# Expert outputs in a mixture-of-experts kernel: stored to rows of their own and fetched back, in place of adding in memory

## What is computed

```python
def moe_swiglu(h, w_router, w1, w3, w2):
    logits = (h @ w_router).astype(jnp.float32)
    top_val, top_idx = lax.top_k(logits, TOP_K)              # TOP_K = 2 of N_EXPERTS = 8
    top_w = jax.nn.softmax(top_val, axis=-1)
    combine = jnp.sum(jax.nn.one_hot(top_idx, N_EXPERTS) * top_w[..., None], axis=-2)
    out = jnp.zeros_like(h)
    for e in range(N_EXPERTS):
        out = out + combine[..., e:e + 1] * swiglu(h, w1[e], w3[e], w2[e])   # 1024 -> 3584 -> 1024
    return out
...
    x = x + moe_swiglu(h, moe_router[i], moe_w1[i], moe_w3[i], moe_w2[i])
return rms_norm(x, final_g)
```

## Time and profile before

| | |
|---|---|
| median of three runs | 1801.39 us (1799.99 to 1801.99) |
| the profiled execution | 1801.36 us, of which the span 1799.5 us |
| busy in the span | PE 1773.1 us (99%), DVE 1520.6 us (85%), ACT 1222.8 us (68%), POOL 82.7 us (5%) |
| moved | 519.87 MB, mean 289 GB/s |

### The profile page before, as it was taken

How to read it: one execution, slowest core, us unless ns; L and a number is a source line. 1 busy time by engine, 2 the same in 40 slices (tenths; PEclk the granted TensorE clock), 3 DMA queues, 4 the chain that set the end, 5 groups by cost and what they waited for, 6 DMA issues and landing times.

```text
span 1799.5 us, 24857 instructions
## 1 busy us (share of the span) xinstructions
PE 1773.1 (99%) x10081; PEld 1528.1 (85%) x10082; DVE 1520.6 (85%) x1408; ACT 1222.8 (68%) x1138; POOL 82.7 (5%) x97
## 2 busy tenths in 40 slices
PE   9999999999999999999999999999999999999997
PEld 9989898899999989898888877887878877787775
DVE  7999866566557999876579889999999999999996
ACT  5657754454445557754577688888788888888886
POOL 1000000100001000000100010001010010000000
PEclk9999999999999999999999999999999999999998
DMA  8543555345554554454379999999999999999995
GB/s 343 180 173 142 186 188 187 118 164 211 186 182 157 194 178 141 169 223 170 111 284 370 356 414 414 428 426 420 426 404 428 425 422 415 416 427 427 421 414 217
DMA packets 55826, 519.87 MB, mean 289 GB/s; under 512 B 7136, under 2 KB 7392, under 8 KB 12320
## 3 DMA queue, kind: packets, MB, share of 16 engines
q1 hardware_dynamic: 52448, 507.83, 71.1%
q0 software_dynamic: 2544, 9.18, 1.7%
q10 hardware_dynamic: 720, 1.31, 0.2%
HBM read 511.74 MB, written 6.55 MB: 288 GB/s over the span
## 4 chain that ended last, share of the span: by engine, by line
PE 79%; DVE 12%; ACT 4%; DMA 3%; issue 2%; SPq 0%; ACTq 0%; DVEq 0%
PE psum L2119 15%; PE psum L2105 13%; PE psum L2106 12%; PE psum L2107 12%; PE psum L2120 8%; PE psum L2607 6%; PE psum L2608 6%; DVE raw_alias L1355 4%; DVE U_alias L1355 2%; DMA raw<-in_stream 2%; ACT whi L816 2%; DVE wlo L1355 2%; DMA U<-in_stream 1%; PE psum L2620 1%; PE psum L2626 1%
## 5 line engine op out<-in xcount | busy, mean ns | idle before, releaser
L816 ACT ACTIVATE whi<-raw 128x2048 fp32r<-128x2048 f32 (+1 forms) x231 | 436.4, 1897 | 93.1 <-PE psum L2120 50.0
L1355 DVE TENSOR_TENSOR wlo<-raw,whi 128x2048 fp32r<-128x2048 f32 (+1 forms) x144 | 326.2, 2266 | 131.5 <-ACT whi L816 131.2
L2119 PE MATMUL psum<-h_hl,whi 128*128 128x512 f32 x1216 | 429.9, 398 | 0.3 <-DVE U L1713 0.2
L2120 PE MATMUL psum<-h_hl,wlo 128*128 128x256 f32 x1216 | 340.0, 280 | 0.0
L2119 PEld LDWEIGHTS psum<-h_hl,whi 128*128 128x128 f32 x1216 | 228.2, 188 | 55.0 <-issue 1.2
L2120 PEld LDWEIGHTS psum<-h_hl,wlo 128*128 128x128 f32 x1216 | 229.4, 189 | 0.1
L1355 DVE TENSOR_TENSOR raw_alias<-raw,wlo 128x2048 fp32r<-128x2048 f32 x87 | 196.6, 2284 | 18.6 <-ACT wlo L816 18.4
L2105 PE MATMUL psum<-act_hl,whi 128*128 128x256 f32 x720 | 206.2, 286 | 1.1 <-DVE wlo L1355 0.5
L1355 DVE TENSOR_TENSOR raw_alias<-raw,whi 128x2048 fp32r<-128x2048 f32 x87 | 196.6, 2285 | 10.1 <-ACT whi L816 9.7
L2106 PE MATMUL psum<-act_hl,whi 128*128 128x256 f32 x720 | 203.7, 283 | 0.0
L2107 PE MATMUL psum<-act_hl,wlo 128*128 128x256 f32 x720 | 203.6, 283 | 0.0
(11 more groups left out here) (326 smaller groups left out, 3365.4 us busy)
## 6 DMA issues: line engine op xcount, KB each, us to landing
raw<-in_stream SPq DMA_DIRECT2D x87, 2048.0 KB, 18.7
raw<-in_stream SPq DMA_DIRECT2D x141, 1024.0 KB, 4.9
U<-in_stream SPq DMA_DIRECT2D x52, 2048.0 KB, 17.6
memhat<-in_stream SPq DMA_DIRECT2D x29, 1024.0 KB, 14.5
h_hl_alias<-in_stream SPq DMA_DIRECT2D x29, 1024.0 KB, 16.4
raw<-in_stream SPq DMA_DIRECT2D x6, 512.0 KB, 3.5
xacc<-U POOLq DMA_DIRECT2D x3, 512.0 KB, 9.8
xT<-in_x_cols ACTq DMA_DIRECT2D x4, 256.0 KB, 6.5
```

What stands on the lines that cost most here:

```text
L816: act.activation(hi_home(n)[:, 0:words], src[:, 0:words], ACT.Copy).then_inc(hi_ready, 1)
L1355: dve.tensor_tensor(lo_home(n)[:, 0:words], src[:, 0:words], hi_home(n)[:, 0:words].bitcast(F32), ALU.subtract).then_inc(lo_ready, 1)
L2119: pe.matmul(o[:].rearrange("p (a b) -> p a b", a=2), st[0], mv, start=start, stop=False)
L2120: return pe.matmul(o[:, 0:256], st[1], mv[:, 0, :], start=False, stop=stop)
```

## The change

- **Stores.** An expert's rows go plainly to rows of its own in a new array `ys` (1 + 7 x 128 rows). Indices past the end mark empty slots, which `bounds_check` leaves out, in the gathers too. Row 0 is zero. `ys` is cleared by seven transfers of 512 KB that ACT issues at chunks 30 to 36 of layer 1, and one of 4 KB at row 0. The three sends of x to `xacc`, `x_rows` and the first calls of `xrows` are gone.
- **Sums.** `rows_listed` (DVE, n = 16) makes a list `yidx` of four columns: for both blocks of 128 tokens the row of a token's later and earlier expert among p = 0 to 6 (or row 0). `sums_in` gathers two times 128 rows by it, once into `xa` when p = 5 has been sent and once into `xsum` after the store of p = 6 has been issued and has landed. PE turns x of tokens 0 to 127 to rows after step 53, and DVE adds them to `xa` (`kept_added`, n = 323 and 324); x of tokens 128 to 255 is added by PE in `final_rows`, in eight more transposes. DVE adds `xsum` to `xa` in four pieces at n = 325 to 328 (`halves_added`), the first of which waits for the second fetch. `final_rows` and ACT wait for these.
- **Order.** `ALONE` = 5: five big steps, then small and big by turns, then five small. From step 10 on the order is as before.
- **Splits.** Six chunks (`UNDIVIDED`: the first gate chunk of p = 2, 4 and 6 at f = 1 and 4) aren't split: PE takes them as they come in four plain 32-bit matmuls by an unsplit copy of the tokens, `he_full`, and ACT and DVE skip them. So half of the last chunk (`down_last`).
- **Places.** The routing steps move to n = 5, 6, 7, 8, 13, 14, 16 and 21, the slot matrices to 9 to 12, `indices` to step 3. `htok` and `sel` move to the start of `U`, and the two areas of `U` swap roles, so that pair 4 is fetched as soon as the cross attention's scores are done. DVE waits for all of `htok` (`ht_done`) ahead of its first slot matrix.

```diff
-AHEAD = 3
+ALONE = 5
...
-    order, big, small = big[:FSTEPS] + small[:AHEAD], big[FSTEPS:], small[AHEAD:]
-    for pair in zip(big, small):
+    order, big = big[:ALONE], big[ALONE:]
+    for pair in zip(small, big):
         order += pair
...
-    return 4 if s >= FSTEPS else 5
+    return 4 if s >= ALONE else 5
...
+UNDIVIDED = [MOE + gate_end(s) - 1 for s in range(STEPS) if ORDER[s][0] and not few_step(s) and ORDER[s][1] % 3 == 1]
...
+def divided(n):
+
+    return n + 1 - sum(i < n for i in UNDIVIDED)
...
-        htok = u(4096, TB, D)
-        sel = u(6144, TB, NE, SLOTS)
+        htok = u(0, TB, D)
+        sel = u(2048, TB, NE, SLOTS)
...
-        PAIRED = {4: 0, JOINING: 2 * CW}
+        PAIRED = {4: 2 * CW, JOINING: 0}
...
+            sp.wait_ge(xs_done, XH * LAYERS)
+            fetch(4, 0)
...
                 elif q == LOOSE:
+                    sp.wait_ge(w_used, MOE)
+                    fetch_loose(q, 1, 0)
...
-                    sp.wait_ge(ss_done, 6)
-                    sp.wait_ge(ht_done, 4)
+                    continue
...
-                if q == 4:
-                    sp.wait_ge(w_used, MOE)
-                    fetch_loose(LOOSE, 1, 0)
...
-            for t in range(TB):
-                gp.wait_ge(xt_ready, 2 * t + 2)
-                gp.dma_start(xacc[P * t:P * t + P, :], xtok).then_inc(scr_in, 16)
-            gp.dma_start(xacc[S:S + SLOTS, :], xtok).then_inc(scr_in, 16)
...
-                  .then_inc(hg_in, 16)
+                                      in_offset=bass.IndirectOffsetOnAxis(ap=gidx[0:there, p:p + 1], axis=0),
+                                      bounds_check=S - 1, oob_is_err=False).then_inc(hg_in, 16)
+
+            def sums_in(to, first):
+
+                for b in range(TB):
+                    at = first + b
+                    gp.indirect_dma_start(out=to[:, b, :], out_offset=None, in_=ys,
+                                          in_offset=bass.IndirectOffsetOnAxis(ap=yidx[:, at:at + 1], axis=0)).then_inc(xa_in, 16)
...
-                    gp.wait_ge(scr_in, 48)
+                    gp.wait_ge(scr_in, 16 * NE)
+                if e == NE - 2:
+                    gp.wait_ge(ga_done, NE)
+                    sums_in(xa, TB)
                 if e < NE - 1:
                     here = HALF if few(e) else SLOTS
                     gp.wait_ge(y_ev, e + 2)
-                    gp.indirect_dma_start(out=xacc, out_offset=bass.IndirectOffsetOnAxis(ap=sidx[0:here, e:e + 1], axis=0),
-                                          in_=y[0:here, :], in_offset=None, compute_op=ALU.add).then_inc(y_sent, 16)
+                    gp.indirect_dma_start(out=ys, out_offset=bass.IndirectOffsetOnAxis(ap=sidx[0:here, e:e + 1], axis=0),
+                                          in_=y[0:here, :], in_offset=None,
+                                          bounds_check=(NE - 1) * SLOTS, oob_is_err=False).then_inc(y_sent, 16)
                     if e + 3 < NE:
                         rows_in(e + 3)
-            gp.wait_ge(ga_done, NE)
-            gp.dma_start(xa, xacc[0:S, :].rearrange("(b p) d -> p b d", p=P)).then_inc(xa_in, 16)
+            sums_in(xsum, 0)
...
+                    p = n - BASE[1] - CLEARED
+                    if 0 <= p < NE - 1:
+                        act.dma_start(ys[1 + SLOTS * p:1 + SLOTS * p + SLOTS, :].rearrange("p (a b) -> p a b", a=DB),
+                                      ones[:].unsqueeze(1).to_broadcast([P, DB, P])).then_inc(scr_in, 16)
...
+                    if p and k == 0:
+                        act.activation(he_full, got, ACT.Copy)
...
-                    if n == 39:
+                    if n == 37:
...
+                    if MOE + n not in UNDIVIDED:
+                        split(MOE + n)
...
+            def rows_listed():
+
+                some, shape = slice(0, NE - 1), [P, TB, NE - 1]
+                there, at = prod[:, 0:TB, some], prod[:, TB:2 * TB, some]
+                mine(dve.tensor_tensor(there, posp[:, :, some], cap[:, some].unsqueeze(1).to_broadcast(shape), ALU.is_le))
+                mine(dve.scalar_tensor_tensor(at, iota8[:, some].unsqueeze(1).to_broadcast(shape), float(SLOTS),
+                                              posp[:, :, some], op0=ALU.mult, op1=ALU.add))
+                settled()
+                mine(dve.scalar_tensor_tensor(there, posp[:, :, some], 0.0, there, op0=ALU.is_gt, op1=ALU.mult))
+                settled()
+                mine(dve.tensor_tensor(there, there, at, ALU.mult))
+                settled()
+                mine(dve.tensor_reduce(rows_f[:, 0:TB], there, AX.X, ALU.max))
+                mine(dve.tensor_reduce(rows_f[:, TB:2 * TB], there, AX.X, ALU.add))
+                settled()
+                mine(dve.tensor_tensor(rows_f[:, TB:2 * TB], rows_f[:, TB:2 * TB], rows_f[:, 0:TB], ALU.subtract))
+                settled()
+                mine(dve.tensor_copy(yidx[:], rows_f))
+
...
+                dve.tensor_scalar(gidx[:], found[:, :, 0], float(S), None, ALU.add)
...
+                dve.scalar_tensor_tensor(sidx[:], found[:, :, 1], -float(FAR), row_of, op0=ALU.mult, op1=ALU.add)\
+                   .then_inc(ix_ready, 1)
...
+            def kept_added(i):
+
+                t, at = i // 2, slice(512 * (i % 2), 512 * (i % 2) + 512)
+                if i == 0:
+                    dve.wait_ge(xa_in, 16 * TB)
+                dve.wait_ge(xt_done, i + 1)
+                dve.tensor_tensor(xa[:, t, at], bank[4 + i][:], xa[:, t, at], ALU.add).then_inc(xt_ready, 1)
+
+            def halves_added(i):
+
+                t, at = i // 2, slice(512 * (i % 2), 512 * (i % 2) + 512)
+                dve.wait_ge(xa_in, 32 * TB)
+                dve.wait_ge(xt_ready, 2)
+                dve.tensor_tensor(xa[:, t, at], xsum[:, t, at], xa[:, t, at], ALU.add).then_inc(xa_sum, 1)
...
+                dve.wait_ge(ht_done, 4)
...
-                routing = {5: ranked, 7: counted, 9: placed, 11: shares, 13: shares_placed, 15: listed, 33: places}
+                routing = {5: ranked, 6: listed, 7: counted, 8: placed, 13: shares, 14: shares_placed, 16: rows_listed, 21: places}
                 for n in range(SPLIT, TOTAL):
                     if n in routing:
                         routing[n]()
-                    if n in (17, 19, 21, 23):
-                        b, odd = divmod((n - 17) // 2, 2)
+                    if n in (9, 10, 11, 12):
+                        b, odd = divmod(n - 9, 2)
...
+                    if n in (323, 324):
+                        kept_added(n - 323)
+                    if n in (325, 326, 327, 328):
+                        halves_added((2, 3, 0, 1)[n - 325])
                     if n == TOTAL - 1:
                         hidden_turned(STEPS - 1)
-                    split(MOE + n)
+                    if MOE + n not in UNDIVIDED:
+                        split(MOE + n)
...
                     counts()
-                elif 1 < f < 5:
-                    if f == 2:
...
+                    indices()
                 elif f == 5:
-                    indices()
-                elif f == 6:
                     last_turned()
...
+            def gate_undivided(n, o):
+
+                words, arrived, value = landed(n)
+                pe.wait_ge(arrived, value)
+                for k in range(4):
+                    ins = pe.matmul(o, he_full[:, P * k:P * k + P], words[:, 512 * k:512 * k + 512], start=k == 0, stop=False)
+                ins.then_inc(w_used, 1)
...
+            def down_last(n0, s):
+
+                words, arrived, value = landed(n0)
+                pe.wait_ge(arrived, value)
+                for o in range(2):
+                    pe.matmul(bank[y_bank(NE - 1) + o][:], eT_few[s % 2][:, 2, :].bitcast(F32), words[:, 512 * o:512 * o + 512],
+                              start=False, stop=False)
+                pe.wait_ge(lo_ready, divided(n0))
+                for o in range(2):
+                    ins = two(bank[y_bank(NE - 1) + o][:], eT_few[s % 2][:, 3, :], wt(n0, 1, D, 512 * o, 512), False, True)
+                    ins.then_inc(w_used if o else y_first, 1)
...
                     at = 512 * (i % 2)
+                    pe.wait_ge(xa_sum, (2, 3, 0, 1).index(i) + 1)
                     pe.matmul(final_bank(0, i // 2, i % 2), ident[:], xa[:, i // 2, at:at + 512],
                               start=True, stop=False, skip_group_check=True)
+                    if i > 1:
+                        for k in range(4):
+                            c = 4 * (i % 2) + k
+                            pe.matmul(final_bank(0, 1, i % 2)[:, P * k:P * k + P], xT[:, c, P:S], ident[:],
+                                      start=False, stop=False, skip_group_check=True)
...
-                        pe.wait_ge(xa_in, 16)
-                        pe.wait_ge(st_ready, 1)
                         for i in (2, 3):
...
                         if ORDER[s - 2][1] == 0:
                             pe.wait_ge(y_ev, max(1, ORDER[s - 2][0]))
```

(6 more changed lines are left out.)

121 lines of the change are left out of this document (58 added, 63 removed).

## The result

The changed kernel takes 1814.09 us in the median (four runs, 1811.93 to 1817.99), against 1801.69 before in the same comparison. The ratio is 1.0067, with a 95% interval of 1.0052 to 1.0082. The forecast was 1793.8, in a range of 1785 to 1802, so it missed in size and sign.

What follows compares the result with a forecast made beforehand. Transfers were taken to bound the expert stage from 1066 us on. Terms summing to -10.0 us put the last store's issue at 1720.4; a 71.5 us tail and 1.9 around the span gave 1793.8 us, range 1785 to 1802.

Steps and rivals of the forecast that it cites:

- What bounds the stage: Expert stage from 1066 us on: transfers bound, and PE has some 25 us to spare in all.
- Stores -8.6: Before the last store: plain stores of real rows only take 3.8 us of transfers in place of 12.4.
- gathers -1.9: Token-row gathers of p = 1 to 7: leaving out empty slots saves 0.79 MB, 1.9 us.
- first fetch +2.6: Ahead of the last store: fetching 2 x 128 rows, 1.05 MB, adds 2.6 us.
- Order -3.5: Expert stage: small steps among big ones earlier let transfers run ahead, gaining 3.5 us (0 to 5).
- Loss of slack +1.4: Expert stage: unsplit chunks use PE's slack and finite homes keep some savings back, costing 1.4 us (0 to 5).
- The tail +2.4: Last store to end: 71.5 us against 69.1, with DVE waiting 5 us for the second fetch; -2.5 to +7.
- B2: Expert stage: PE or DVE take over as the bound, no lead from the order; 1800.9 us, chance 0.12.
- A: Tail: the second fetch lands in time, so DVE has no wait for it; 1788.9 us, chance 0.17.
- B1: GpSimd's queue: skipped slots cost what written ones do; 1797.6 us, chance 0.12.
- C: Tail: the second fetch's two gathers go one after the other, DVE stands for 22 us; 1810.6 us, chance 0.09.
- The rule beside it: Gathers under load: the skill's fit estimates 3.2 us for 0.5 MB; the trace before disagrees, median 13.2 us.

Runs made afterwards that it cites:

- the first experiment: The kernel before with its seven stores to xacc made plain (no adding, empty slots left out): 1795.62 us against 1802.82, ratio 0.9962.
- the second run: The changed kernel with the list UNDIVIDED empty, so all gate chunks are split: 1808.04 us, ratio to the kernel before 1.0034.
- fourth run: The changed kernel with the order of steps as before the change: 1813.28 us, ratio to the kernel before 1.0059.

## Why the prediction was wrong, step by step

**What bounds the stage** was the step that failed first: "from 1066 us on the transfers bound, PE has about 1 us to spare per pair of steps". The prediction took 29.4 us of the matrix engine for a pair of steps, which the rows of the first experiment bear out (29.5), and 29.5 of the stream with about 1 of GpSimd's queue, 30.4, for the transfers. That looks right beside the measured mean of 30.5 (seven pairs in the 213.65 us between the stores at 1306.30 and 1519.95). But the matrix engine has more to do than in a plain pair. The seven pairs between two stores of big experts take 29.5 us twice, and 30.0, 30.7, 30.7, 30.9 and 31.9 us. One of the 30.7 and the 30.9 hold turns of the next experts' rows, and the 31.9 holds a wait of 1.4 us for VectorE. The lengths are the same to about 0.05 us with plain stores and in the second run, and at most 0.3 more before. Their mean is 30.5. The reserve of 25 us on the matrix engine was not there; over 497 us, 0.6 us of it was.

**Stores -8.6, gathers -1.9, first fetch +2.6.** Together they came to between 0 and -0.7. The transfers went as priced (9.7 us less in the queue by its share, the stretch holding part of the tail too), but the plain stores alone and the change without unsplit chunks have the last store 0.6 and 0.2 us earlier, and the stretch between the second and the last store 0.6 and 0.7 us shorter.

**Order -3.5** isn't borne out (fourth run); at most about 1 us of it can be hidden in that run's trace. The 4% of free share before 1066 us were not time that anyone waited for to any such amount.

**Loss of slack +1.4.** An unsplit chunk was priced at 0.72 us of the matrix engine. The second of an expert's two costs 0.75, the first about 0.3, by the lengths of their pairs. What was wrong was to set the 4.3 us against slack. With no slack the six cost 3.1 us by X and 6.0 in the medians.

**The tail +2.4** was +6.8. The mechanism was right: VectorE waits at its first addition, with everything queued behind it. The sizes were off, and each on the short side. The store landed after 9.1 us (8.5 taken), and the gathers after 19.4 us from the first one's issue (16.8), the time to landing of the two being

```profile
DMA to landing us min/median/max: 13.2/14.7/16.2
```

so L was X + 29.9, inside its bounds of 24.6 to 31. From L on it took 46.0 us (44.9). So of the 4.4 us more than forecast, 3.3 are the later L and 1.1 come after it; there the lower clock after the longer wait (0.50 for five us) is a part that no run took by itself.

**Rivals.** B2, that PE or DVE take over, was nearest in mechanism for the part before X; it is PE that had it all along. It was priced at 1800.9 because its bound for the lost slack, 5 us, still let 2.9 of the 7.9 us saved through. All but 0.7 of them were lost, and the unsplit chunks come on top. A was false by 10 us of landing. B1 was not tested by itself, and no longer matters where transfers don't count. C, the only one on the slow side, needed L = X + 38 and got X + 29.9. The change became slower at a smaller L because X didn't move: 1730.4 + 3.1 + 29.9 + 46.0 = 1809.4, the span measured (1810.2) within 1 us; the rest is the later start of the layer.

**The rule beside it.** A gather of 0.5 MB by the fit of the Trainium skill, "DMA: Bandwidth & Descriptors", section on the anatomy of one DMA, was estimated at 3.2 us. Here the two had 13.2 and 16.2 under the stream's load, so the measurement decides against the fit there. The same page's account of queues served by turns, in its section on queues and completion order, fits a gather that the stream stretches, but no run here shows the turns.

## What to carry to other kernels

A DMA share near 1.0 doesn't say that transfers bound. Look for whether the engine at the end of the chain ever waits for them, or take transfers away in one kernel and watch a milestone deep in the stage before counting on a gain. Measure between two milestones inside the stage: such a stretch repeated to 0.1 us in 497, where the totals of one kernel scattered by several us. Work out an engine's own time from every kind of step, not from the plain one, before giving it slack. When engine and transfers are matched to about a us in 500, take nothing off one of them for credit and put nothing on either: a saving of some 10 us was worth 0.6, an addition of 9 in bursts cost 18. A wait put on an engine that splits for the matrix engine brings idle time and then a stretch at the lower clock, so it goes behind the work that can still be done, four splits later here.
